# Layer 1's row normalisation, input projection and query projection put into one program, on one Trainium2 core

## The reference, cut to what matters

```python
h = rms_norm(x, norm_g[1]) * (1 + scale) + shift          # (rows, 1024)
cq, ckv, kr, g = split_cols(h @ c_w_in, (384, 128, 32, 1024))
q = rms_norm(cq, q_norm_g) @ c_w_uq                       # (rows, 16 heads * 96)
q_rope, kr = apply_rope(q[..., 64:], pos), apply_rope(kr, pos)
ckv = rms_norm(ckv, kv_norm_g)                            # outputs: ckv, kr
# attention over ckv and kr, then  x = x + gate * ((o * silu(g)) @ c_w_out)
```

## Time and profile before

| | us |
|---|---|
| timed runs | 2097.89, 2097.42, 2093.26 (median 2097.42) |
| profiled execution, its own time | 2087.48 |
| its span, first to last instruction | 2085.7 |
| PE busy | 1727.8 (83%) |
| DVE busy | 1298.8 (62%) |
| ACT busy | 951.9 (46%) |
| POOL busy | 236.5 (11%) |
| mean granted TensorE clock | 0.904 |

### The profile page before, as it was taken

One profiled execution on the slowest core, in us unless ns is written; L12 is line 12 of the kernel. 1 busy time (PEld: TensorE's weight loads), 2 busy tenths in 40 slices (PEclk: granted clock), 3 DMA queues, 4 the chain that ended last, 5 costly groups with the idle time before them and its releaser, 6 DMA issues. The chain is left out here.

```text
span 2085.7 us, 34359 instructions
## 1 busy us (share of the span) xinstructions
PE 1727.8 (83%) x12754; PEld 1335.0 (64%) x12754; DVE 1298.8 (62%) x2840; ACT 951.9 (46%) x1886; POOL 236.5 (11%) x328
## 2 busy tenths in 40 slices
PE   5693488999998976899997964979794999999787
PEld 2461256888876854677775753758683777667566
DVE  2632464887999944688885425341394777777554
ACT  4311352224511364678872125368432776767211
POOL 5000100000000102111100000010003232220000
PEclk8795687999999987999998986989897999999899
DMA  7464602442234219987735331231245111110522
GB/s 275 157 197 137 115 2 81 101 127 81 75 78 106 86 46 226 233 227 201 201 89 190 123 151 49 67 97 46 75 99 129 33 26 42 26 33 9 191 94 99
DMA packets 235806, 230.46 MB, mean 110 GB/s; under 512 B 148037, under 2 KB 171877, under 8 KB 233594
## 3 DMA queue, kind: packets, MB, share of 16 engines
q1 hardware_dynamic: 226170, 198.91, 35.9%
q0 software_dynamic: 9472, 29.36, 3.8%
HBM read 173.98 MB, written 54.23 MB: 109 GB/s over the span
## 5 line engine op out<-in xcount | busy, mean ns | idle before, releaser
L410 PE MATMUL PS<-ab_wh,hT 128*128 128x512 f32 x576 | 229.1, 398 | 10.5 <-DVE ab_wl L610 9.9
L412 PE MATMUL PS<-ab_wh,hT 128*128 128x512 f32 x576 | 225.4, 391 | 0.0
L411 PE MATMUL PS<-ab_wl,hT 128*128 128x512 f32 x576 | 225.0, 391 | 0.0
L1046 DVE TENSOR_SCALAR_CACHE_REDUCE topk_junk<-scores,topk_small 128x528 bf16<-128x528 f32 (+6 forms) x224 | 194.5, 915 | 1.3
L2115 DVE CUSTOM_DVE_ANT_0 la_S<-PS,la_mask 128x128 f32<-128x128 f32 (+3 forms) x144 | 107.5, 747 | 38.7 <-PE PS L412 25.4
L410 PEld LDWEIGHTS PS<-ab_wh,hT 128*128 128x128 f32 x576 | 108.7, 189 | 33.2 <-ACT ab_wh L542 6.5
L410 PE MATMUL PS<-out_wh,out_mT 128*128 128x512 f32 x288 | 118.9, 413 | 10.5 <-DVE out_wl L1605 10.0
L1392 ACT ACTIVATE at_P<-at_S,at_nm 128x128 f32<-128x128 f32 (+2 forms) x144 | 110.4, 767 | 30.7 <-DVE at_nm L1437 30.6
L412 PEld LDWEIGHTS PS<-ab_wh,hT 128*128 128x128 f32 x576 | 108.6, 189 | 23.4
L411 PEld LDWEIGHTS PS<-ab_wl,hT 128*128 128x128 f32 x576 | 108.9, 189 | 21.4
L411 PE MATMUL PS<-out_wl,out_mT 128*128 128x512 f32 x288 | 115.9, 403 | 0.0
(11 more groups left out here) (427 smaller groups left out, 4529.6 us busy)
## 6 DMA issues: line engine op xcount, KB each, us to landing
ab_w<-in_ab_w_in SPq DMA_DIRECT2D x64, 256.0 KB, 2.9
out_g<-scratch_gates_nat SPq DMA_DIRECT2D x18, 512.0 KB, 6.0
mod_ada_w<-in_ada_w SPq DMA_DIRECT2D x8, 1024.0 KB, 12.7
mod_w<-in_ada_w SPq DMA_DIRECT2D x16, 512.0 KB, 5.0
mod_w<-in_ada_w SPq DMA_DIRECT2D x8, 1024.0 KB, 6.1
at_kc<-in_cache_a_k SPq DMA_DIRECT2D x8, 1024.0 KB, 10.0
at_vc<-in_cache_a_v SPq DMA_DIRECT2D x8, 1024.0 KB, 7.7
at_kc<-in_cache_b_k SPq DMA_DIRECT2D x8, 1024.0 KB, 7.9
```

What stands on the lines that cost most here:

```text
L410: nc.tensor.matmul(out, x[0], w[0], start=start, stop=False)
L411: nc.tensor.matmul(out, x[0], w[1], start=False, stop=False)
L412: return nc.tensor.matmul(out, x[1], w[0], start=False, stop=stop)
L1046: go(V.tensor_scalar(mark, x, limit, 0.0, op, ALU.add, accum_out=cnt[:, m:m + 1]), 0 if m == M - 1 else 1)
```

## The change

`Norm` and `normed_rows` go. In their place a class `Front` does its work tile by tile inside the first call of `projection`, which now has all eight groups, in the order latent, narrow, query 0, gate 0, query 1, gate 1, query 2, query 3. A group is an object with its own operand, weights and weight slot (four slots instead of two).

- SP fetches the latent group's first four weight tiles and row tiles 0 and 1 at the end of layer 0's output projection. The other rows come through two buffers: row i is loaded once row i-2 is turned.
- POOL scales the rows, in place of ACT: rows 0 and 1 first, then row s+2 ahead of the store of step s.
- PE turns rows 0 and 1 first, then row s+2 ahead of the product of step s, always into PSUM banks 6 and 7. ACT and DVE evict row s+2 ahead of their work for step s.
- The query groups wait once for `kept_lo` (all nine tiles of `cqT`).
- `across` (the narrow group's buffer) now lies in `tmp`.
- In `mixed_out`, both layers, the prompt's gate vector keeps a buffer; the sample rows' one goes into slot 1 of the weight ring, and `ms` into slot 0. SP therefore waits for all eight weight splits before it issues the sample gate and all that stands behind it.

```diff
+class Front:
+
+    loaded = 4
+
+    def __init__(self, nc, c, stack):
+        self.nc, self.c = nc, c
+        S = lambda n: semaphore(nc, f"norm1_{n}")
+        self.x_in, self.w_in = [S("x_in0"), S("x_in1")], [S(f"w_in{r}") for r in range(RING)]
+        self.std, self.rstd_done, self.scaled, self.tr_done = S("std"), S("rstd"), S("scaled"), S("tr")
+        self.h_done, self.h_act, self.mid_done, self.hi_done, self.lo_done = S("h"), S("h_act"), S("mid"), S("hi"), S("lo")
+        sb = lambda n, shape: stack.enter_context(nc.sbuf_tensor(f"norm1_{n}", shape, F32, side="right"))
+        self.x, self.w, self.rstd = sb("x", [P, 2, D]), sb("w", [P, RING, 512]), sb("rstd", [P, NT])
+
+    def enter(self, stack):
+        self.h = stack.enter_context(self.nc.sbuf_tensor("norm1_h", [P, 2, KT, P], F32))
+
+    def fetch(self, sp, i):
+        sp.dma_start(self.x[:, i % 2, :], self.c.s["x1"][i * P:(i + 1) * P, :]).then_inc(self.x_in[i % 2], 16)
+
+    def fetch_weights(self, sp, w_dram, col, n):
+        for r in range(self.loaded):
+            sp.dma_start(self.w[:, r, 0:n], w_dram[r * P:(r + 1) * P, col:col + n]).then_inc(self.w_in[r], 16)
+
+    def load(self, sp, i):
+        if i < NT:
+            sp.wait_ge(self.tr_done, 2 * (i - 1))
+            self.fetch(sp, i)
+
+    def begin_act(self, act):
+        self.nc.scalar.activation(self.rstd[:], self.c.ss1[:], ACT.Sqrt, scale=1.0 / D, bias=self.c.eps[:]).then_inc(self.std, 1)
+
+    def begin_dve(self, dve):
+        dve.wait_ge(self.std, 1)
+        self.nc.vector.reciprocal(self.rstd[:], self.rstd[:]).then_inc(self.rstd_done, 1)
+
+    def scale(self, pool, i):
+        if i >= NT:
+            return
+        if i == 0:
+            pool.wait_ge(self.rstd_done, 1)
+        pool.wait_ge(self.x_in[i % 2], 16 * (i // 2 + 1))
+        row = self.x[:, i % 2, :]
+        self.nc.gpsimd.tensor_scalar(row, row, self.rstd[:, i:i + 1], None, ALU.mult).then_inc(self.scaled, 1)
+
+    def turn(self, pe, i):
...
+        pe.wait_ge(self.scaled, i + 1)
+        for half in range(2):
+            if i:
+                pe.wait_ge(self.h_act if half else self.h_done, 4 * i)
+            for q in range(4):
+                k = 4 * half + q
+                last = self.nc.tensor.transpose(self.c.PS[:, 6 + half, q * P:(q + 1) * P], self.x[:, i % 2, k * P:(k + 1) * P], self.c.ident[:])
+            last.then_inc(self.tr_done, 1)
+
+    def wait_tile(self, pe, i):
+        pe.wait_ge(self.hi_done, i + 1)
+        pe.wait_ge(self.lo_done, i + 1)
+
+    def act(self, act, i):
+        if i >= NT:
+            return
+        nc, m = self.nc, self.c.modT
+        if i < QT:
+            act.wait_ge(self.tr_done, 2 * i + 2)
+            if i >= 2:
+                act.wait_ge(self.lo_done, i - 1)
+            for q in range(4):
+                k = 4 + q
+                nc.scalar.activation(self.h[:, i % 2, k, :], self.c.PS[:, 7, q * P:(q + 1) * P], ACT.Identity, scale=m[:, 1, 0, k, 0:1],
+                                     bias=m[:, 1, 1, k, 0:1]).then_inc(self.h_act, 1)
+            act.wait_ge(self.h_act, 4 * i + 4)
+        act.wait_ge(self.h_done, 4 * i + 4 if i < QT else 4 * QT + KT)
+        nc.scalar.activation(self.hT[0][:, :, i * P:(i + 1) * P], self.h[:, i % 2], ACT.Copy).then_inc(self.hi_done, 1)
+
+    def low(self, dve, i):
...
+            dve.wait_ge(self.tr_done, 2 * i + 1)
+            if i >= 2:
+                dve.wait_ge(self.lo_done, i - 1)
+            for q in range(4):
+                nc.vector.tensor_scalar(self.h[:, i % 2, q, :], self.c.PS[:, 6, q * P:(q + 1) * P], m[:, 1, 0, q, 0:1], m[:, 1, 1, q, 0:1],
+                                        ALU.mult, ALU.add).then_inc(self.h_done, 1)
+        else:
...
-            for r in range(kt + RING - 1):
+            for r in range(front.loaded if front else 0, groups[0].kt + RING - 1):
                 load_w(sp, r)
+            if front:
+                front.load(sp, 2)
+                front.load(sp, 3)
...
-                        load_w(sp, kt * (steps[s][0] + 1) + k + RING - 1)
+                        load_w(sp, first[steps[s][0] + 1] + k + RING - 1)
+                if front:
+                    front.load(sp, s + 4)
...
         def _(pool):
             counts = [0] * 4
+            for i in range(2 if front else 0):
+                front.scale(pool, i)
             for s, (g, i) in enumerate(steps):
-                if groups[g][3]:
+                if front:
+                    front.scale(pool, s + 2)
+                if groups[g].nat:
                     pool.wait_ge(nat_done, s + 1)
-                    for d, src in groups[g][3](i, nat[:, s % 4, :]):
+                    for d, src in groups[g].nat(i, nat[:, s % 4, :]):
                         pool.dma_start(d, src).then_inc(nat_out[s % 4], 16)
                         counts[s % 4] += 16
...
+                front.begin_act(act)
+            for k in range(groups[0].kt):
                 split_high(0, k)
+                if front and k % 4 == 3:
+                    front.act(act, k // 4)
             for s in range(len(steps) + LAG):
                 if s < len(steps):
+                    if front:
+                        front.act(act, s + 2)
...
+            for i in range(2 if front else 0):
+                front.turn(pe, i)
             for s in range(len(steps) + LAG):
                 if s < len(steps):
                     g, i = steps[s]
-                    n = groups[g][1]
+                    n = groups[g].n
+                    if front:
+                        front.turn(pe, s + 2)
+                        if s < NT:
+                            front.wait_tile(pe, s)
...
+                    if groups[g].kind == "qc" and g == min(q for q in range(len(groups)) if groups[q].kind == "qc") and i == 0:
+                        pe.wait_ge(kept_lo, NT)
...
+        ms, sample_gate = w[:, 0, :].rearrange("p (a b) -> p a b", a=KT), w[:, 1, :]
...
-            sp.dma_start(gate[:, 0, :], dram(c.s["gate"], l * NR * D, [[0, P], [1, D]])).then_inc(rows_in, 16)
-            sp.dma_start(gate[:, 1, :], dram(c.s["gate"], (l * NR + 1) * D, [[D, NB], [0, TS], [1, D]])).then_inc(rows_in, 16)
+            sp.dma_start(gate[:], dram(c.s["gate"], l * NR * D, [[0, P], [1, D]])).then_inc(rows_in, 16)
+            sp.wait_ge(w_lo, KT)
+            sp.dma_start(sample_gate, dram(c.s["gate"], (l * NR + 1) * D, [[D, NB], [0, TS], [1, D]])).then_inc(rows_in, 16)
             if last_layer:
                 sp.dma_start(fg[:], dram(c.i["final_norm_g"], 0, [[0, P], [1, D]])).then_inc(rows_in, 16)
             for i in range(2, NT):
                 rows(i)
+            if front:
+                front.fetch_weights(sp, c.i["c_w_in"][0], 0, QL + KVL)
+                for i in range(2):
+                    sp.wait_ge(stored[i], 16)
+                    front.fetch(sp, i)
...
+        front.hT = hT
+        w_c, w_q, n = c.i["c_w_in"][0], c.i["c_w_uq"][0], 4 * (NOPE + RD)
+        cq = [cqT[:, 0], cqT[:, 1]]
+        latent = Group(hT, KT, w_c, 0, QL + KVL, "latent", lambda i, src: [(tile_of(o["p_c_latent"], o["s_c_latent"], i), src[:, QL:QL + KVL])],
+                       lambda i: [c.s["latT"][d].rearrange("(a p) t -> p a t", p=P)[:, :, i * P:(i + 1) * P] for d in range(2)], 1.0,
+                       lambda i: [cqT[:, d, :, i * P:(i + 1) * P] for d in range(2)], slot=0)
+        krope = Group(hT, KT, w_c, QL + KVL, RD, "krope", lambda i, src: [(tile_of(o["p_c_krope"], o["s_c_krope"], i), src[:, 0:RD])],
+                      lambda i: [c.s["krT"][d][:, i * P:(i + 1) * P] for d in range(2)], 1.0, slot=1)
+        gate = [Group(hT, KT, w_c, QL + KVL + RD + 512 * a, 512, "silu", gates(512 * a), slot=0) for a in range(2)]
+
+        def queries(g):
+            turned = lambda i: [c.s["qcT"][d, 4 * g:4 * g + 4, :, i * P:(i + 1) * P].rearrange("h p t -> p h t") for d in range(2)]
+            return Group(cq, QL // P, w_q, n * g, n, "qc", None, turned, C_SCALE, slot=2 + g % 2)
+        projection(nc, c, "c", [latent, krope, queries(0), gate[0], queries(1), gate[1], queries(2), queries(3)], front=front)
...
+        with ahead, nc.sbuf_tensor("hT1", [P, 2, KT, TOK], F32R) as pair:
             hT = [pair[:, 0], pair[:, 1]]
-            with ExitStack() as inner:
-                norm = Norm(nc, c, 1, lambda i: c.s["x1"][i * P:(i + 1) * P, :], inner, c.ss1)
-                normed_rows(nc, c, 1, norm, hT)
-            latent_projection(nc, c, hT)
+            latent_projection(nc, c, hT, front)
```

More of the change, by code:

```diff
@@ L323, in normed_rows @@
-def normed_rows(nc, c, l, norm, hT):
-    with (nc.sbuf_tensor(f"h{l}", [P, 2, KT, P], F32) as hm, nc.sbuf_tensor(f"h_mid{l}", [P, KT, P], F32) as mid,
-          nc.Block() as block):
-        @block.sync
-        def _(sp):
-            norm.load(sp)
-        @block.scalar
-        def _(act):
-            norm.scale(act)
-        @block.vector
-        def _(dve):
-            norm.invert(dve)
```

(26 more changed lines are left out.)

210 lines of the change are left out of this document (95 added, 115 removed).

## The result

The change costs time. The changed kernel takes 2103.93 us (median of 15 runs, 2095.10 to 2116.69) against 2095.67 for the kernel before (15 runs, 2080.54 to 2098.95); the ratio is 1.0065 with a 95% interval of 1.0037 to 1.0093. The forecast was 2122, range 2102 to 2142. The profiled executions took 2087.48 and 2096.92 us (spans 2085.7 and 2095.2).

The account below looks back on a forecast made before the run. TensorE, with VectorE also pacing the query groups, was taken to bound the kernel, apart from row normalisation and two gaps. Terms 2.2 - 24.5 + 59.5 - 1.1 - 2 - 10 + 1 = +25.1 us gave 2122, range 2102 to 2142.

Parts of the forecast that it names:

- Step 3: Latent group: a loop of product, norm, store, scale, turn stalls six steps at 15.8 us; +59.5, first product -1.1.
- lower bound: Latent group: the loop's period with turn and product both at the high clock, 13.2 us.
- Step 2: From layer 0's output projection to the first product: 29.1 us instead of 53.6, -24.5 (-29 to -18).
- Steps 1 and 6: Output projections of layers 0 and 1: the sample gate's load waits for all weight splits; +2.2 and +1.
- Step 4: Narrow group: it splits three weight tiles of 384 columns instead of eight of 512; -2 (-5 to 0).
- Step 5: Query groups between gate groups: one program removes the gap before the queries; -10 (-16 to -3).
- C: Rival: latent steps grow by the turn alone, since the scale is ready; sum -29.4, 2068 us; chance 0.12.
- B: Rival: the clock stays low through the latent group, period 18.9; +46.8, 2144 us; chance 0.10.
- D: Rival: VectorE and GpSimd exclude each other, so low splits wait for scales; +4.6 more, 2127 us; chance 0.05.
- 0.2 where they meet: Latent group: the cost in us to VectorE's low-part subtraction beside GpSimd's scale, inside other work.

Follow-up runs that it names:

- d: The changed kernel with 14 extra, unread matmuls ahead of the turn in six stalled latent-group steps; 2101.34 us, 1.0056 against the kernel before.
- a: The changed kernel with GpSimd scaling each row one step sooner, row s+3 ahead of the store of tile s; 2066.57 us, ratio 0.9884.
- g: The kernel before with only the changed output projection (mixed_out), nothing fetched ahead; 2102.93 us, ratio 1.0038.
- i: The changed kernel with scale one step sooner, sample gate loaded behind the last row tile, and gate rows requested two tiles ahead; 2030.59 us, 0.9724.
- l: The kernel before with only each tile's gate rows requested two tiles ahead in both output projections; 2074.02 us, ratio 0.9911.
- e: The kernel before with its eight groups merged in one program, keeping the separate row phase and old output projection; 2078.85 us, ratio 0.9935.
- f: The kernel before with eight groups merged in one program, both gate groups placed before all query groups; 2073.73 us, ratio 0.9904.
- k: The changed kernel with scale one step sooner, sample gate last, gate rows two tiles ahead, product before turn, rows 2 and 3 requested sooner; 2021.11 us.
- b: The changed kernel with the sample rows' gate loaded behind row tile 2 and waited for only before the last row tile; 2109.71 us, ratio 1.0097.
- c: The changed kernel with scale one step sooner and the sample rows' gate loaded behind row tile 2; 2057.59 us, ratio 0.9849.
- h: The changed kernel with scale one step sooner and the sample gate loaded behind the last row tile; 2050.77 us, ratio 0.9808.

## Why the prediction was right, and where its terms were off

It named the loop, its place and its price, and the direction follows from it. The total is another matter: the median was forecast to rise by 24.6 us and rose by 8.3, and 2103.9 lies 1.9 above the lower end of the range. The fair test is the sum over the stages, +25.1 forecast and +20.5 measured. Point by point:

**Step 3, the latent group: right.** Forecast +58.4 for group and first product, measured +55.1. The period was forecast at 15.8, from eight matmuls at the low clock in every step. Steps with eight measured 15.68 to 15.83, the steps between, with three, 14.76 to 15.17, the mean is 15.35. So the mis-sized term is the slow part of every second product, 2.7 us over six steps. The lower bound holds too: d reached 13.24 at the high clock. That a store ahead of the scale makes the loop is shown by a, which moves only that.

**Step 2, the start: -24.5 forecast, -27.5 measured.** The mis-sized term is the load of row 2, taken at 6.1 us from a gate row's load under traffic. SyncE issued it at 1245.23 and the scale began at 1248.69:

```profile
1245.23 0.91 SPq L377 DMA_DIRECT2D norm_x<-scratch_x  x2
...
1248.69 3.15 POOL L402 TENSOR_SCALAR norm_x<-norm_x,norm_rstd 128x1024 f32<-128x1024 f32 x1 [8.24 <-DMA norm_x<-scratch_x]
```

That is 3.5 us: the same 0.5 MB took little more than half as long here. Both loads had another one of 0.5 MB issued within half a microsecond of them, and why they differ stays open. The forecast's own sum has a slip, too: its parts add up to 23.8 (12.8 + 6.1 + 2.84 + 2.1), not 24.4. The rest of the path was as told: the request came 12.9 us after the block's first instruction (ScalarE's table load at 1232.32), forecast 12.8.

**Steps 1 and 6, the output projections: +3.2 forecast, +7.9 measured** (+6.2 by the means over the profiles with the same code). The mechanism was right (g shows it), both sizes too small. In layer 0:

```profile
1109.65 0.62 SPq L1605 DMA_DIRECT2D out_w<-scratch_gate  x1
...
1117.28 1.23 DVE L1682 TENSOR_TENSOR mix<-mix,out_rinv 128x1024 f32<-128x1024 f32 x1 [7.66 <-DMA out_w<-scratch_gate]
```

The load took 7.6 us, not 6.1, and the wait grew by 3.6, not 2.2. The next gate rows are requested 0.7 us behind this load; whether they slow it down was not tested. In layer 1 VectorE resumes 9.0 us after its last split, 6.5 before:

```profile
1973.59 1.23 DVE L1682 TENSOR_TENSOR mix<-mix,out_rinv 128x1024 f32<-128x1024 f32 x1 [8.98 <-DMA out_fg<-in_final_norm_g]
```

The forecast's phrase that the loop has "nothing to spare, so it stays late" was right, though it was said of layer 0 only; i and l bear it out. I had it correctly there and denied it in the expectation for i.

**Step 4: -2 forecast, -3.6 measured. Step 5: -10 forecast, -10.3 measured.** e confirms both together (-12.3). The parts of step 5 came out close as well: the first query group takes 21.9 us (forecast 20.5), the second 23.6 (24). But the reason is the joint alone; the order, which the forecast priced together with it, earns nothing (f).

**Sum.** +25.1 was forecast for the stages, +20.5 measured; the start gave 3 more than forecast, the latent group 3, the narrow group and attention 1.6 and 1.0, and the projections took 4.7 back. The forecast of 2122.5 lies 18.6 above the measured median. Of that 4.6 are these terms, 11.0 the code ahead of the change (last section), and 2.9 that the median lies 7.0 above the profiled execution and not 9.9. So most of the miss in the total is not in the changed stages; it is what brought the total down to the lower end of the range.

**The rivals.** C had its chance at 0.12: its step, longer by the turn alone (6.0 + 1.1), is what a shows when the scale stands one step sooner (7.13). In the stages a gains 26.8 us against C's 29.4; that the medians agree so closely, 2066.6 and 2068, is partly chance, since the projections cost more and the code ahead of the change took another time. B fell: the granted clock was 0.81 and the period 15.35, not 18.9. D would have let the first four low splits wait for two scales. It rests on the Trainium skill ("SBUF — State Buffer", section "Who interferes with whom"), which says that a VectorE instruction with two SBUF inputs contends with a GpSimd one that reads SBUF and calls the shared port pair an exclusive lock; that the other waits for the whole instruction it says of VectorE's two-port modes. The changed kernel has four splits beside the scale, and four without it:

```profile
1234.47 3.26 DVE L689 TENSOR_TENSOR c_wl<-norm_w,c_wh 128x512 fp32r<-128x512 f32 x4 [0.30 <-ACT c_wh L615]
...
1242.95 2.49 DVE L689 TENSOR_TENSOR c_wl<-norm_w,c_wh 128x512 fp32r<-128x512 f32 x4
```

They start 0.2 us into the first scale (1234.27 to 1237.12) and are done at 1237.73, so they did not wait for two scales. All of the 0.8 us that they lose is in the first, 1.45 us long; the other three take 0.68, as without a scale. In the latent group a much smaller subtraction loses more, beside the scale of 1310.40 shown above:

```profile
1310.44 1.13 DVE L689 TENSOR_TENSOR c_wl<-norm_w,c_wh 128x32 fp32r<-128x32 f32 x1
```

Two tiles before, at 1278.52, with no scale beside it, the same takes 0.18. The three sizes fit one reading: a subtraction of two SBUF tiles that starts early in a scale ends as if it had started 0.97 to 1.0 us into it (0.20 + 1.45 - 0.68; 0.04 + 1.13 - 0.18; and 0.76 + 1.43 - 1.22 in the opening), while one that starts 1.3 us into it or later is not slowed. So here there is a hold, but it covers about the first third of the scale's 2.85 us, and the forecast's 0.2 where they meet is right only for what starts 0.76 us into it. One scale does not fit, in k: it is 3.58 us long, a split 0.26 us into it is not slowed, and one 0.87 us into it takes 1.52. Why the hold ends there is not shown. None of this stands in the loop's path.

## What to carry to other kernels

Writing a call two steps ahead does not make it run ahead: an engine issues in order, so ask what the instruction ahead of it on its queue waits for, and walk round from there; if the walk comes back to the start, the sum of it is the period. The same holds for a DMA queue. A load that nobody needs soon cost some 3 or 6 us in layer 0, or nothing that could be told, by what stood behind it, and loads that a loop waits for belong ahead of the queue's own waits. Price a change from stages, above all when the stages around it can move by as much.

## What was not expected of the hardware

The 11.0 us ahead of the change start in a loop that both kernels have, the index scores of layer 0. From 290 to 330 us, before and changed:

```profile
290.00:330.00 40.00, 37.42 (x106) 25.06 (x107) 7.90 (x11) 11.06 (x18) 0.00 (x0) 0.53 0.00 0
```

```profile
290.00:330.00 40.00, 30.81 (x122) 21.57 (x123) 12.60 (x18) 15.55 (x25) 0.00 (x0) 0.79 0.15 46
```

The granted clock is 0.53 in the one and 0.79 in the other, with TensorE busier at the lower clock. The next program's first weights are requested at 335.1 and 321.6 us. In the profiles of all fourteen kernels that clock is 0.50 to 0.62 in ten and the request at 330 to 336, and 0.70 to 0.79 in four (changed, a, b, d) with the request at 321 to 326. Kernels with the same front (c, h to k) stand on the other side, so the change alone does not decide it. But none of the five kernels without the front has the higher clock, and four of the nine with it have; whether the front makes it more frequent is not shown. What tips it was not found; nor do these up to 15 us account for all of the spread, as the time from there to layer 0's projection also varies, from 761 to 774. For both reasons the measured ratio (8 us) is smaller than what the change costs in its stages (20.5), and only stages were compared above.
